# Two edits to an encoder kernel: the turns of one pair's probabilities stand ahead of the next pair's scores on TensorE, and the copies of the turned probabilities wait for the values of the pair before

## The chip, the core and the metric

The kernel runs on one core of a Trainium2 chip. TensorE (PE in the profile) multiplies matrices, PEld is its weight load, VectorE (DVE) and ScalarE (ACT) work on tiles in on-chip memory and on the accumulator banks, GpSimd (POOL) does a few small operations, and SyncE (SP) issues most of the DMAs. The metric is the device time of one execution in microseconds (us), lower is better.

## What is computed

The reference is a two-layer encoder trunk for 256 positions of width 1024 in float32. Cut to what matters here:

```python
for l in range(DEPTH):                       # DEPTH = 2
    x = x + 0.5 * swiglu(rmsnorm(x, g_ff1[l]), w1_ff1[l], w3_ff1[l], w2_ff1[l])
    h = rmsnorm(x, g_mix[l])
    p = h @ w_in[l]                          # queries, keys, values of three branches, and three gates
    o_a = diff_attention(...)                # 4 heads: softmax(s0) - lam * softmax(s1), then values, then a norm
    o_b = neighborhood_attention(...)        # 8 heads
    o_c = dilated_attention(...)             # 8 heads
    g = sigmoid(gates)
    merged = g[0] * (o_a @ w_br_a[l]) + g[1] * (o_b @ w_br_b[l]) + g[2] * (o_c @ w_br_c[l])
    x = x + merged @ w_o[l]
    x = x + 0.5 * swiglu(rmsnorm(x, g_ff2[l]), w1_ff2[l], w3_ff2[l], w2_ff2[l])
return rmsnorm(x, g_final)
```

Each attention is scores, a bias, a softmax over 256 keys, and the product of the probabilities with the values.

## The kernel before

All weights come as a stream of 1 MB units of 128 x 2048 numbers. To keep float32 precision, ScalarE copies each unit to a rounded high part (`to_hi`, L445, `whi`), VectorE subtracts it from the original to get the low part (`to_lo`, L1102, `wlo`), and TensorE forms each product from three matmuls, high by high, high by low and low by high (`three`, L679 to L681). Three units are in flight. The order of the instructions on each engine is written out by hand, and semaphores are all that joins the engines. Each engine works through its list strictly in that order.

The change lies in the mixing stage, which each layer runs once. Its loop over `j` has one unit per step: `MIX` lists 18 of them (gates and branch projections), four output units follow. Beside the units of steps 0 to 13 the stage handles the attention in 12 pairs of heads: pairs 0 to 3 are the dilated branch C, 4 to 7 the neighbourhood branch B, and 8 to 11 the differential branch A (there one "pair" is one head with its two softmaxes). TensorE's step `j` before the change is:

- the unit of the step (`unit_rows`, 24 matmuls of 512 columns),
- `scores(j)`: the scores of pair j into banks 2 and 3,
- `values(j - 2)`: the product of the turned probabilities of pair j-2 with its values,
- `turn_probs(j - 1)`: the transposes of pair j-1's normalised probabilities into banks 4 and 5 (eight transposes, four for each head of the pair; four in all for a pair of branch A).

ScalarE's step `j` has, in this order: in some steps two gate activations (L617); `pair_to_hi(j + 1)` (L564, `hTh_last`, waits for the end of `scores(j)`, since it writes the tiles that they read); `to_hi` of a unit three steps ahead (L445); the copies of pair j-1's turned probabilities (L629, `pTh`, two for branches C and B, one for A); the high part of pair j-1's values (L634, `hTh`); and the four exponentials of pair j (L641, `probs`). VectorE's step `j` has: in some steps work on the branch products; `add_bias(j)` (L1326); the low part of pair j+1 (L1255); the low parts of the turned probabilities of pair j-1 (L1353, `pTl`) and of its values (L1356); `to_lo` of the unit (L1102); the reciprocal of pair j's softmax sums (L1393); and the normalisation of pair j's probabilities (four of L1399, the first two for the first head; for branch A two of L1406 and two of L1410). The transposes of a head wait for its normalisation (`normed`, or `mixed` for A), and those of pairs 1 to 8 for the low parts of the pair before (`pT_split`), which still read the same banks.

`values(j - 2)` reads the copies of pair j-2. The copies of pair j-1 overwrite them. Before the change they wait for `probs_turned` alone, which TensorE raises behind the values.

Of the kernel before, what the change touches and what calls it, by code (L numbers as in the profile page):

```python
# [46 lines left out]
PAIRS = 12  # L47
# [50 lines left out]
def build(nc, x_in, stream, params_in, lam_in, g_final, t5_table, rpb, c_ident, c_mask, c_onehot, c_lncount, out):  # L98
    with ExitStack() as ctx:
# [117 lines left out]
        def n_norm(l, j):  # L217
            return l * 3 + (j + 1)
# [213 lines left out]
        def _(act):  # L432
# [138 lines left out]
            for l in range(DEPTH):  # L571

                later_quarters(l, 0, U_FFN1 + 2)
                ffn(l, 0, U_FFN1, 0, 1)

                later_quarters(l, 1, U_QKV + 2)
                act.wait_ge(rstd_ready, n_norm(l, 1))

                def branch(b):
                    for p in range(3):  # L580
                        u = U_QKV + 2 * p
                        to_hi(l, u + 3, b * 2)
                        if p == 0:
                            for t in range(TILES):
                                if t == 0:
                                    act.wait_ge(half_done, n_unit(l, u + 1, b * 2))
                                else:
                                    act.wait_ge(unit_used, n_unit(l, u + 1, b * 2) + CREDIT)
                                act.activation(v[:, b, t, :], v_bank(b, t)[:, :], ACT.Copy, scale=rstd[:, 0, t:t + 1]).then_inc(v_out, 1)
                        else:  # L590
                            for blk in range(BLK):
                                if blk == 0:
                                    act.wait_ge(half_done, n_unit(l, u + 1, b * 2))
                                elif blk == 2:
                                    act.wait_ge(unit_used, n_unit(l, u + 1, b * 2) + CREDIT)
                                half = qk_bank(b, p - 1, blk)[:, S:2 * S]
                                act.activation(qkT[:, b, p - 1, blk, :], half if p == 1 else half[:, ::-1], ACT.Copy).then_inc(qk_half, 1)
                        to_hi(l, u + 4, b * 2)

                branch(0)  # L600
                act.wait_ge(setup_done, 4)
                act.wait_ge(t5_stored, 16)
                pair_to_hi(l, 0)
                for b in (1, 2):
                    branch(b)
                act.activation(warm[:, :], factors[:, 0, :], ACT.Exp)

                for j in range(len(MIX) + 4):
                    u = U_MIX + j
                    kind, b, n, a = MIX[j] if j < len(MIX) else ("wo", 0, 0, 0)  # L610
                    if kind == "gate" and a == 1:
                        for t in range(TILES):
                            if t == 0:
                                act.wait_ge(half_done, n_unit(l, u))
                            else:
                                act.wait_ge(unit_used, n_unit(l, u) + CREDIT)
                            act.activation(gate[:, b % 2, t, n * 512:(n + 1) * 512], bank[t][:, :], ACT.Tanh,  # L617
                                           scale=rstd[:, 1, t:t + 1]).then_inc(gate_ready, 1)
                    if j < PAIRS - 1:
                        pair_to_hi(l, j + 1)  # L620
                    for inst, q in QUARTERS_AT.get(j, []):
                        quarter(l, inst, q)
                    due = split_at(u) if j < len(MIX) + 3 else []
                    for w in due[:1]:
                        to_hi(l, w)
                    if 1 <= j <= PAIRS:
                        for m in range(2 if j <= 8 else 1):
                            act.wait_ge(probs_turned, n_probs_turned(l, j - 1, m))
                            act.activation(pTh[:, m, :, :] if j <= 8 else pTa[:, :, :], bank[4 + m][:, :].rearrange("p (a b) -> p a b", a=2),  # L629
                                           ACT.Copy).then_inc(pT_hi, 1)  # L630
                    if 1 <= j <= 8:
                        if j > 1:
                            act.wait_ge(pv_done, l * 12 + j - 1)
                        act.activation(map_columns(vh[:, :, :]), v_of_pair(j - 1), ACT.Copy).then_inc(v_hi, 1)  # L634
                    if j < PAIRS:
                        if j >= 1:
                            act.wait_ge(probs_turned, n_probs_turned(l, j - 1, 0 if j - 1 >= 8 else 1))
                        for m in range(2):
                            act.wait_ge(biased, l * 24 + 2 * j + m + 1)
                            for t in range(TILES):  # L640
                                e = act.activation(probs[:, m, t, ::-1], sneg[:, m, t, :], ACT.Exp, scale=-1.0,  # L641
                                                   bias=negmax[:, m, t:t + 1], accum_out=den[:, m, t:t + 1])
                            e.then_inc(exp_done, 1)
                    for b2, half in OT_AT.get(j, []):
                        if b2 == BA:
                            act.wait_ge(o_turned, l * 2 + half + 1)
                        else:
                            act.wait_ge(pv_done, l * 12 + 4 * b2 + 2 * half + 2)
                        if b2 == BB:
                            act.wait_ge(unit_used, n_unit(l, U_MIX + 9) + CREDIT)  # L650
                        dst, src = o_parts(b2, half)[0], o_turns(b2, half)
                        act.activation(dst, src, ACT.Copy, **({"scale": params[:, l, SUBLN:SUBLN + 1]} if b2 == BA else {})).then_inc(o_hi, 1)
                    for w in due[1:]:
                        to_hi(l, w)

                later_quarters(l, 3, U_FFN2 + 2)
                if l == DEPTH - 1:
                    act.dma_start(gate[:, 0, 0, :], bass.AP(g_final.tensor, 0, [[0, P], [1, D]])).then_inc(gfin_landed, 16)
                ffn(l, 1, U_FFN2, 2, NEXT)
# [16 lines left out]
        def _(pe):  # L676
# [240 lines left out]
            for l in range(DEPTH):  # L917
# [58 lines left out]
                def turn_probs(s):  # L976
                    b = s // 4
                    if 1 <= s <= 8:
                        pe.wait_ge(pT_split, l * 16 + 2 * s)
                    elif s:  # L980
                        pe.wait_ge(pT_hi, n_probs_turned(l, s - 1, 0))
                    for m in range(1 if b == BA else 2):
                        if b == BA:
                            pe.wait_ge(mixed, l * 4 + (s - 8) + 1)
                        else:
                            pe.wait_ge(normed, l * 16 + 2 * s + m + 1)
                        for kb in range(TILES):
                            for t in range(TILES):
                                last = pe.transpose(bank[4 + m][:, kb * S + t * P:kb * S + (t + 1) * P],  # L989
                                                    probs[:, m, t, kb * P:(kb + 1) * P], ident[:, :])  # L990
                        last.then_inc(probs_turned, 1)
# [46 lines left out]
                for j, (kind, b, n, a) in enumerate(MIX):  # L1038
                    pr = product_banks(j)
                    before = products_read(j) if j and a == 0 else (None, None)  # L1040
                    if kind == "gate":
                        unit_rows(l, U_MIX + j, 0, xTh, xTl, 4 * a, pr, a == 0, a == 1, before=before)
                    else:
                        if n == 0:
                            pe.wait_ge(o_split, l * 6 + 2 * b + 2)
                        th, tl, k0 = (xTh, xTl, 4) if b == BA else (oTh, oTl, 0)
                        turn_first = (lambda: turn_quarter(l, 2, 0)) if (b, n) == (BA, 1) else None
                        unit_rows(l, U_MIX + j, 0, th, tl, k0, pr, True, True, before=before, mid=turn_first)
                    if j < PAIRS:
                        scores(j)  # L1050
                    if 2 <= j < PAIRS + 2:
                        values(j - 2)
                    if 1 <= j <= PAIRS:
                        turn_probs(j - 1)
                    if j == PAIRS + 2:
                        turn_o(0)
                        turn_o(1)
# [507 lines left out]
```

## Time and profile before

| | |
|---|---|
| median of 3 runs | 1285.77 us (1285.12 to 1286.24) |
| profiled execution | 1284.99 us |
| its span, first to last instruction | 1282.7 us |
| TensorE busy | 1270.0 us (99%) |
| weight load busy | 1082.0 us (84%) |
| VectorE busy | 867.7 us (68%) |
| ScalarE busy | 681.4 us (53%) |
| mixing stage of the first layer with pairs in it | from 298 to 405 us of the span |
| the same of the second layer | from 931 to 1038 us |

In the rows below a time at the start of a row is the start in us from the beginning of the span, the next number is how long the row's instructions took together, and "x8" says that the row stands for eight of them. A matmul's end is modelled, and matmuls overlap, so on TensorE the distance from one start to the next says more than the length of one. A note such as "[0.75 <-ACT pTh L629]" says that the engine sat idle for 0.75 us before the row, until ScalarE had done line L629.

### The profile page before, as it was taken

The page shows a single profiled execution, that of the slowest core. Times are in us where ns is not written, and L with a number is a line of the kernel's source. Part 1 is how long each engine was busy: PE and PEld are TensorE (multiplying, and loading weights), DVE is VectorE, ACT ScalarE, POOL GpSimd, SP SyncE. Part 2 cuts the span into 40 slices and gives each one's busy share as a digit, 9 for nine tenths or more (in the row PEclk, how much of TensorE's full clock was granted, in tenths as well). Part 3 has the DMA queues.
Part 4 walks back from the last instruction along what each step waited for, and adds up shares of the span by engine and source line. Part 5 has one row for each costly group of instructions (what it writes and reads, how often), then busy time and mean ns, then how long its engine had stood idle before and what let it go on. Part 6 is the DMA issues. An engine that isn't in the chain of part 4 may idle for free.

```text
span 1282.7 us, 17691 instructions
## 1 busy us (share of the span) xinstructions
PE 1270.0 (99%) x6825; PEld 1082.0 (84%) x6825; DVE 867.7 (68%) x1236; ACT 681.4 (53%) x919; POOL 42.2 (3%) x56
## 2 busy tenths in 40 slices
PE   8999999999999999999999999999999999999997
PEld 6888888888888888888888888888888888888886
DVE  6666667556988775666676665765578887655665
ACT  6445555445765454544555445554477653645444
POOL 0411100000000000000000000000000000000000
PEclk9999999999999999999999999999999999999999
DMA  8787855564645545555455555455555345555550
GB/s 287 238 258 239 259 212 197 196 214 148 230 122 177 180 179 196 182 183 187 171 194 196 196 184 180 160 211 193 188 195 207 123 171 190 181 197 196 196 191 39
DMA packets 59356, 245.13 MB, mean 191 GB/s; under 512 B 21360, under 2 KB 27760, under 8 KB 32552
## 3 DMA queue, kind: packets, MB, share of 16 engines
q1 hardware_dynamic: 58160, 242.83, 54.6%
q10 hardware_dynamic: 1112, 1.57, 0.4%
q8 instruction: 35, 0.57, 0.2%
q14 instruction: 17, 0.14, 0.0%
q0 software_dynamic: 32, 0.02, 0.0%
HBM read 239.14 MB, written 5.27 MB: 191 GB/s over the span
## 4 chain that ended last, share of the span: by engine, by line
PE 96%; DVE 2%; ACT 1%; DMA 1%; issue 0%; SPq 0%; POOL 0%; POOLq 0%; ACTq 0%; DVEq 0%
PE bank L745 30%; PE bank L679 16%; PE bank L749 15%; PE bank L681 15%; PE bank L680 15%; PE bank L989 1%; PE bank L803 1%; PE bank L1003 1%; DVE wlo L1102 1%; DMA raw<-in_stream 1%; ACT whi L445 0%; PE bank L707 0%; PE bank L699 0%; DVE h L1161 0%; DVE h L1169 0%
## 5 line engine op out<-in xcount | busy, mean ns | idle before, releaser
L1102 DVE TENSOR_TENSOR wlo<-raw,whi 128x2048 fp32r<-128x2048 f32 x209 | 479.1, 2294 | 276.5 <-ACT whi L445 272.6
L445 ACT ACTIVATE whi<-raw 128x2048 fp32r<-128x2048 f32 x209 | 398.7, 1911 | 225.7 <-PE bank L749 142.2
L745 PE MATMUL bank<-xT,whi 128*128 128x512 f32 x1664 | 414.8, 391 | 0.0
L745 PEld LDWEIGHTS bank<-xT,whi 128*128 128x128 f32 x1664 | 301.8, 188 | 55.7 <-DVE wlo L1102 0.9
L749 PEld LDWEIGHTS bank<-xT,wlo 128*128 128x128 f32 x1664 | 220.2, 190 | 12.8
L749 PE MATMUL bank<-xT,wlo 128*128 128x256 f32 x1664 | 224.1, 282 | 0.0
L679 PE MATMUL bank<-whi,xT 128*128 128x512 f32 x432 | 171.7, 397 | 0.0
L681 PE MATMUL bank<-whi,xT 128*128 128x512 f32 x432 | 168.5, 390 | 0.0
L680 PE MATMUL bank<-wlo,xT 128*128 128x512 f32 x432 | 168.3, 390 | 0.0
L679 PE MATMUL bank<-whi,hTh 128*128 128x512 f32 x320 | 124.6, 390 | 0.0
L680 PE MATMUL bank<-wlo,hTh 128*128 128x512 f32 x320 | 124.5, 389 | 0.0
L681 PE MATMUL bank<-whi,hTl 128*128 128x512 f32 x320 | 124.5, 389 | 0.0
L681 PEld LDWEIGHTS bank<-whi,xT 128*128 128x128 f32 x432 | 81.1, 188 | 17.4
L680 PEld LDWEIGHTS bank<-wlo,xT 128*128 128x128 f32 x432 | 81.2, 188 | 16.0
L679 PEld LDWEIGHTS bank<-whi,xT 128*128 128x128 f32 x432 | 81.2, 188 | 15.9
L499 ACT ACTIVATE h<-bank 128x256 f32<-128x256 f32 x80 | 26.4, 382 | 87.8 <-PE bank L745 87.8
L680 PEld LDWEIGHTS bank<-wlo,hTh 128*128 128x128 f32 x320 | 60.1, 188 | 12.8
L679 PEld LDWEIGHTS bank<-whi,hTh 128*128 128x128 f32 x320 | 60.1, 188 | 12.6
L681 PEld LDWEIGHTS bank<-whi,hTl 128*128 128x128 f32 x320 | 60.1, 188 | 12.5
L1161 DVE TENSOR_TENSOR h<-bank,h 128x256 f32<-128x256 f32 x80 | 30.2, 419 | 43.9 <-ACT h L499 43.9
L503 ACT ACTIVATE silu<-silu 128x512 f32<-128x512 f32 x40 | 25.3, 633 | 51.4 <-DVE silu L1164 51.4
L641 ACT ACTIVATE probs<-sneg,negmax 128x256 f32<-128x256 f32 x96 | 47.5, 501 | 0.6 <-DVE negmax L1326 0.6
(162 smaller groups left out, 1139.8 us busy)
## 6 DMA issues: line engine op xcount, KB each, us to landing
raw<-in_stream SPq DMA_DIRECT2D x209, 1024.0 KB, 4.8
bias<-t_rows SPq DMA_DIRECT2D x24, 256.0 KB, 6.5
bias<-in_rpb SPq DMA_DIRECT2D x16, 256.0 KB, 7.7
masked<-bias SPq DMA_DIRECT2D x8, 512.0 KB, 6.9
bias<-masked SPq DMA_DIRECT2D x8, 512.0 KB, 4.7
raw<-in_stream SPq DMA_DIRECT2D x11, 256.0 KB, 7.4
x<-in_x SPq DMA_DIRECT2D x4, 256.0 KB, 6.2
gate<-in_g_final ACTq DMA_DIRECT2D x1, 512.0 KB, 3.6
```

The lines of the kernel that those rows point to most:

```text
L445: act.activation(whi[:, s, :], raw[:, s, :], ACT.Copy).then_inc(hi_ready, 1)
L499: act.activation((h_flat if blk >= 2 else silu_flat)[:, part], bank[4 + blk][:, S:2 * S], ACT.Copy).then_inc(half_copied, 1)
L503: act.activation(silu_flat, silu_flat, ACT.Silu).then_inc(silu_done, 1)
L641: e = act.activation(probs[:, m, t, ::-1], sneg[:, m, t, :], ACT.Exp, scale=-1.0, bias=negmax[:, m, t:t + 1], accum_out=den[:, m, t:t + 1])
L679: pe.matmul(dst, sh, mh, start=start, stop=False)
L680: pe.matmul(dst, sh, ml, start=False, stop=False)
L681: return pe.matmul(dst, sl, mh, start=False, stop=stop)
L745: return pe.matmul(dst[blk][:, :], whi[:, s, w], xT[:, 4 * a + k, :, :].rearrange("p a s -> p (a s)"), start=start, stop=stop)
L749: return pe.matmul(dst[blk][:, 0:S], wlo[:, s, w], xT[:, 4 * a + k, 0, :], start=False, stop=stop)
L803: last = pe.transpose(bank[6 + q % 2][:, k * P:(k + 1) * P], src[:, t, c:c + P], ident[:, :])
L1102: dve.tensor_tensor(wlo[:, s, :], raw[:, s, :], whi[:, s, :].bitcast(F32), ALU.subtract).then_inc(unit_split, 1)
L1161: dve.tensor_tensor(sums, bank[4 + blk][:, 0:S], sums, ALU.add).then_inc(summed, 1)
```

## The change

On TensorE `turn_probs(j - 1)` moves from the end of the step to the place between the unit and `scores(j)`. Since `probs_turned` then no longer says that `values(j - 2)` is done, ScalarE gets one more wait ahead of the copies: from step 2 on it waits until `pv_done` counts the values of pair j-2. Nothing is added or removed on TensorE, VectorE, GpSimd or SyncE.

```diff
@@ scalar, mixing loop @@
                     if 1 <= j <= PAIRS:
+                        if j >= 2:
+                            act.wait_ge(pv_done, l * 12 + j - 1)
                         for m in range(2 if j <= 8 else 1):
                             act.wait_ge(probs_turned, n_probs_turned(l, j - 1, m))
@@ tensor, mixing loop @@
+                    if 1 <= j <= PAIRS:
+                        turn_probs(j - 1)
                     if j < PAIRS:
                         scores(j)
                     if 2 <= j < PAIRS + 2:
                         values(j - 2)
-                    if 1 <= j <= PAIRS:
-                        turn_probs(j - 1)
```

From ScalarE's edit on, every line number of the changed file is two higher.

On TensorE, in step 2 of the first layer, the rows before are these, with repeated rows left out: the last matmul of the unit (reading `xT`), the scores (reading `hTh_last`), the values (reading `pTh`), the eight transposes (reading `ident` and `probs`) and the first matmul of the next unit.

```order
L681 MATMUL bank<-whi,xT 128x512
L679 MATMUL bank<-hTh_last 128x256
L680 MATMUL bank<-hTl_last,hTh_last 128x256
...
L679 MATMUL bank<-pTh,hTh 128x256
L680 MATMUL bank<-pTl,hTh 128x256
...
L989 MATMUL bank<-ident,probs 128x128 x8
L679 MATMUL bank<-whi,xT 128x512
```

In the changed kernel the same place reads as follows.

```order
L683 MATMUL bank<-whi,xT 128x512
L991 MATMUL bank<-ident,probs 128x128 x8
L681 MATMUL bank<-hTh_last 128x256
L682 MATMUL bank<-hTl_last,hTh_last 128x256
...
L681 MATMUL bank<-pTh,hTh 128x256
L682 MATMUL bank<-pTl,hTh 128x256
...
L681 MATMUL bank<-whi,xT 128x512
```

The transposes have moved up past 12 matmuls of the scores and 12 of the values.

On ScalarE the order of the rows is the same. In step 3 of the first layer it is, in the changed kernel: the high part of the next pair, the unit's high part, the two copies of the turned probabilities, the high part of the values, and the exponentials.

```order
L564 ACTIVATE hTh_last<-qkT 128x512 [waits scores_ready]
L445 ACTIVATE whi<-raw 128x2048 [waits raw_landed2,unit_used]
L631 ACTIVATE pTh<-bank 128x512 [waits probs_turned,pv_done]
L631 ACTIVATE pTh<-bank 128x512 [waits probs_turned]
L636 ACTIVATE hTh<-v 128x2x2x64 [waits pv_done]
L643 ACTIVATE probs,den<-sneg,negmax 128x256 [waits biased,probs_turned]
```

Only the first copy has changed: before, its wait was for `probs_turned` alone.

## Rows read from the trace of the kernel before

**Rows 1.** The page: busy us of each engine, share of the span, instructions.

```profile
PE 1270.0 (99%) x6825; PEld 1082.0 (84%) x6825; DVE 867.7 (68%) x1236; ACT 681.4 (53%) x919; POOL 42.2 (3%) x56
```

**Rows 2.** Busy time in the first layer's mixing stage: start:end, length, PE, PEld, DVE, ACT, POOL, granted clock, DMA.

```profile
295.00:405.00 110.00, 110.00 (x674) 92.17 (x672) 92.96 (x257) 78.00 (x168) 0.00 (x0) 1.00 0.51 170
```

**Rows 3.** Timeline of TensorE, steps 4 and 5 of the first layer.

```profile
335.16 0.39 PE L679 MATMUL bank<-hTh_last 64*128 64x256 f32 x2
...
336.07 0.39 PE L679 MATMUL bank<-pTh,hTh 128*128 128x256 f32 x1
...
337.61 1.03 PE L989 MATMUL bank<-ident,probs 128*128 128x128 f32 x8
338.40 0.47 PE L679 MATMUL bank<-whi,xT 128*128 128x512 f32 x1
...
343.72 0.39 PE L681 MATMUL bank<-whi,xT 128*128 128x512 f32 x1
344.04 0.39 PE L679 MATMUL bank<-hTh_last 64*128 64x256 f32 x2
```

**Rows 4.** Timeline of ScalarE in the same stretch.

```profile
336.22 0.63 ACT L564 ACTIVATE hTh_last<-qkT 128x512 fp32r<-128x512 f32 x1 [3.14 <-PE bank L681]
336.75 1.90 ACT L445 ACTIVATE whi<-raw 128x2048 fp32r<-128x2048 f32 x1
338.56 1.07 ACT L629 ACTIVATE pTh<-bank 128x512 fp32r<-128x512 f32 x2
```

**Rows 5.** Timeline of VectorE in the same stretch.

```profile
339.17 1.29 DVE L1353 TENSOR_TENSOR pTl<-bank,pTh 128x512 fp32r<-128x512 f32 x2 [0.75 <-ACT pTh L629]
...
343.11 1.14 DVE L1399 TENSOR_SCALAR probs<-probs,rden 128x256 f32<-128x256 f32 x4
```

**Rows 6.** Timeline of TensorE and VectorE, step 4 of the second layer.

```profile
968.97 0.39 PE L679 MATMUL bank<-pTh,hTh 128*128 128x256 f32 x1
976.01 1.15 DVE L1399 TENSOR_SCALAR probs<-probs,rden 128x256 f32<-128x256 f32 x4
```

**Rows 7.** Timeline behind the first feed-forward stage: TensorE waits for VectorE.

```profile
451.24 1.28 DVE L1133 SCALAR_TENSOR_TENSOR x<-bank,x 128x512 f32<-128x512 f32 x2
452.10 0.59 PEld L803 LDWEIGHTS bank<-ident,x 128*128 128x128 f32 x4
452.33 0.60 PE L803 MATMUL bank<-ident,x 128*128 128x128 f32 x4
```

**Rows 8.** Timeline of VectorE and TensorE, steps 0 to 2 of the first layer.

```profile
307.67 1.14 DVE L1399 TENSOR_SCALAR probs<-probs,rden 128x256 f32<-128x256 f32 x4
310.89 1.09 PE L989 MATMUL bank<-ident,probs 128*128 128x128 f32 x8
317.93 1.14 DVE L1399 TENSOR_SCALAR probs<-probs,rden 128x256 f32<-128x256 f32 x4
```

**Rows 9.** Timeline of TensorE, steps 8 to 11 of the first layer: the values' first matmuls, and turns.

```profile
371.59 0.39 PE L679 MATMUL bank<-pTh,hTh 128*128 128x256 f32 x1
...
380.47 0.39 PE L679 MATMUL bank<-pTh,hTh 128*128 128x256 f32 x1
...
388.91 1.16 PE L1003 MATMUL bank<-v,silu 128*128 128x128 f32 x8
389.91 0.60 PE L989 MATMUL bank<-ident,probs 128*128 128x128 f32 x4
...
396.82 1.16 PE L1003 MATMUL bank<-v,silu 128*128 128x128 f32 x8
```

**Rows 10.** Timeline of VectorE, steps 8 to 11: the second half of branch A's normalisation.

```profile
379.41 0.88 DVE L1410 SCALAR_TENSOR_TENSOR probs<-probs,lrden 128x256 f32<-128x256 f32 x2
...
386.24 0.88 DVE L1410 SCALAR_TENSOR_TENSOR probs<-probs,lrden 128x256 f32<-128x256 f32 x2
...
395.26 0.88 DVE L1410 SCALAR_TENSOR_TENSOR probs<-probs,lrden 128x256 f32<-128x256 f32 x2
...
402.56 0.88 DVE L1410 SCALAR_TENSOR_TENSOR probs<-probs,lrden 128x256 f32<-128x256 f32 x2
```

## Prediction

> **What bounds the kernel now.** I read the page first. TensorE is busy for 1270.0 us of the 1282.7 us span [rows 1]. Then the busy time of the stage that the change touches: in 110 us of the first layer's mixing stage TensorE is busy for 110.00, VectorE for 92.96 and ScalarE for 78.00, at a granted clock of 1.00, the 2.4 GHz level [rows 2]. So nothing that waits today is waited for by TensorE, and the change takes no work off it. It can only add waits on TensorE, or save the small losses between one kind of matmul and the next. The question is therefore when the normalised probabilities are ready, against the new, earlier place of their transposes. For that I went through the timeline of the three engines step by step.
>
> Some names. S is the start of the first instruction behind a step's scores on TensorE, in most steps the first matmul of the values. N is the end of the normalisation of the first head of the same pair. In step 4, S is 336.07 [rows 3]. VectorE starts the four normalisations at 343.11, and they take 1.14 together [rows 5]; one is about 0.35 long and they start 0.265 apart (0.35 + 3 x 0.265 = 1.14), so the first two end at 343.11 + 0.61 = 343.72, and the second two 0.53 later. N - S is 343.72 - 336.07 = 7.65.
>
> What sets these 7.65 us? ScalarE makes the next pair's high part right when the scores are done, 0.15 after S (336.22, after 3.14 idle). It takes a unit's high part at 336.75, and the copies of the turned probabilities start when that is done, at 338.56 [rows 4]. VectorE sits idle for 0.75 until the first copy is there, and then works through low parts, a unit's low part and the reciprocal up to the normalisation [rows 5]. So the chain starts from the end of the scores, and it is in the order of the two engines' lists, not in the turns: when ScalarE reaches the copies the turns are just done. The whole chain hangs on S and moves with it.
>
> **The change, part by part.** Nothing is added to or taken from TensorE's work. The transposes of pair j move up to a place right behind the unit of step j+1. How long after S does TensorE reach that place? Values: 337.61 - 336.07 = 1.54. The unit's 24 matmuls: the first starts at 338.40 and the 24th at 343.72, which is 23 steps of 0.23, so the next can start at 343.95, 5.55 later [rows 3]. TensorE arrives at S + 7.09. The first head's probabilities are there at S + 7.65, later. In the kernel before, the scores and values of step j+1 lie in between, and the turns start 2.45 us later than the unit's end (scores 336.07 - 335.16 = 0.91, values 1.54 [rows 3]); this is what hid the chain.
>
> What does the engine lose on top when it really waits? The row of a wait for VectorE elsewhere: two residual sums take 1.28 together (about 0.68 each, overlapping), the first ends at 451.92, the weight load of the turn that waits for it starts at 452.10 and its first matmul at 452.33 [rows 7]. That is 0.41 from the end of the VectorE instruction. The two bounds are 0.18 (only the way of the signal, if the load is hidden) and 0.41; I take 0.41, since a turn loads its own data and that row is the same kind of wait. The second head's four turns could start at N + 0.41 + 0.40 (eight take 0.79 [rows 3]), but their data end at N + 0.53, and 0.41 on top is N + 0.94: another 0.13.
>
> Now each pair of a layer:
> - Pair 0: its first step has no values and no copies, so it is normalised at 307.67 + 1.14 = 308.81. Its turns stand at 310.89 now, behind 0.91 of scores; at 309.98 they find everything ready [rows 8]. 0.
> - Pair 1: S was 310.89, the start of the turns then in that place, and N is 317.93 + 0.61 = 318.54 [rows 8], again 7.65. There are no values in step 1, so TensorE arrives after the unit alone: 7.65 + 0.41 + 0.13 - 5.55 = 2.64 us.
> - Pairs 2 to 7, six of them: 7.65 + 0.41 + 0.13 - 7.09 = 1.10 each, 6.60 in all.
> - Pair 8, the first of branch A: its normalisation has two stages, the last of which ends at 379.41 + 0.88 = 380.29; S is 371.59 [rows 9, 10], so 8.70. One wait only: 8.70 + 0.41 - 7.09 = 2.02.
> - Pair 9: 386.24 + 0.88 - 380.47 = 6.65 [rows 9, 10]; with 0.41 it is 7.06, just under the 7.09. 0.
> - Pair 10: 395.26 + 0.88 - 388.91 = 7.23. The values of branch A are shorter, 389.91 - 388.91 = 1.00 [rows 9, 10], so TensorE arrives at 6.55: 7.23 + 0.41 - 6.55 = 1.09.
> - Pair 11: 402.56 + 0.88 - 396.82 = 6.62 [rows 9, 10]: 6.62 + 0.41 - 6.55 = 0.48.
>
> The sum is 12.83 us a layer. The second layer reads the same: in its step 4 the chain is 976.01 + 0.61 - 968.97 = 7.65 [rows 6]. So 25.7 us.
>
> The waits don't pile up on one another, and none pays for the next: behind each the scores follow, a new S starts a new chain of the same length, and TensorE again has 7.09 us of work for it. Nothing behind the stage can give the time back, since TensorE is never waiting there for anything that this delay would hide.
>
> ScalarE's new wait costs nothing by these rows: the values now end 1.54 after S, and ScalarE reaches the copies 2.49 after S (338.56 - 336.07 [rows 3, 4]), so there is 0.95 to spare, 0.77 after the 0.18 that a signal takes. What hides it is the copy of the unit's high part, which ScalarE does from 0.68 to 2.49 after S; without that it would wait about 1 us (0.68 against 1.72). Queued behind it are the exponentials, and with them the normalisation. The transposes also wait for the low parts of the pair before, but those are made ahead of the normalisation on VectorE's list, so they are never last. SyncE's loads wait for units that are freed; with TensorE slower there is only more room.
>
> The small losses between kinds of matmuls: 0.32 instead of 0.23 from the unit's last matmul to the scores [rows 3], so 0.09 there, and the like behind a turn. Turned differently, they may save or cost about 0.1 a step, at 12 steps and two layers up to 2.4 us either way. I take 0, since in most steps TensorE is waiting at just that place.
>
> **The clock.** The granted clock was at the upper level in this stage, with TensorE never idle in it [rows 2]. Now it will be idle for about 1 us of every 10, and no row here shows what follows from that. The Trainium skill (page "TensorE: Matmul & The Clock Gate", section "HAM oscillation — how this bites in real kernels") says that pauses between bursts of matmuls can bring the clock down to its lower level. By that rule the stage would run at the price of the third rival below; by the rows it costs 25.7 us.
>
> **Rivals.** First, the chain gets shorter, and nothing changes. The exponentials of pair j wait for the turns of pair j-1, and the copies too. If it is the turns that ScalarE waits for, they come 2.45 us earlier, N - S falls well under 6.68 (7.09 - 0.41, the point from which it decides), and almost no wait is left: N - S would be 5.20, which leaves 5.20 + 0.54 - 5.55 = 0.19 at pair 1 and nothing elsewhere, 1286 us. Against it: the copies start right behind the unit's high part [rows 4], not behind the turns. Second, the other side: no waits, and the small losses fall away since turns follow a unit and the values lead into the next one. With 0.09 saved at both places in 11 steps of two layers that is 22 x 0.18 = 4.0, so 1282 us. It needs the same condition, N - S below 6.68, at each pair. Third, the clock goes to 1.2 GHz in the stage. A step would then have 2 x 7.09 = 14.2 us of work beside the chain, no wait, and with turns and scores (2 x 1.7) be 17.6 long in place of 8.9: some 8.7 x 22 = 190 us, 1475 us. Fourth, the waits are there, but without the 0.23 of the first load and the 0.13 of the second head: 12.83 - 10 x 0.23 - 7 x 0.13 = 9.6 a layer, 19 in all, 1304 us.
>
> **How the numbers follow.** The forecast, waits of the size above: 0.72. The cheaper waits (fourth): 0.16. No change (first): 0.06. Faster (second): 0.03. Clock (third): 0.02. The remaining 0.01 I leave to anything else that is slower. The sum stands against the profiled execution's 1284.99: 1284.99 + 25.7 = 1310.7. The median of the runs is 0.8 above that execution, so 1311.5, and I say 1311. For the range I go from the cheap waits with 2.4 saved between kinds, 1285.8 + 19.2 - 2.4 = 1302.6, to 1311.5 + 2.4 and a little for waits that are not listed, 1315: 1302 to 1315, which leaves out less than 2 in 10. 0.2% of this kernel's time, about 2.6 us, is what a measurement can tell from no change. Faster by more than that 0.03, within it 0.06, slower 0.91.
>
> **What would show it.** In the profile after, TensorE's list of waits should have the turns of `probs` waiting for VectorE's normalisation, about ten times a layer, the longest in step 2 (some 2.5 us) and step 9 (some 2), about 1 us in steps 3 to 8, and hardly any in steps 1 and 10. N - S should still be 7.65. A step in the middle should be about 10.0 us from scores to scores where it was 344.04 - 335.16 = 8.88 [rows 3], TensorE's clock should stay at 1.00, and ScalarE should not be waiting for the values at its copies, except in step 9. The prediction is wrong if N - S shrinks, if TensorE's re-entry after a wait is far from 0.41, or if the clock drops.

## The result, and the profile after

The changed kernel takes 1309.94 us (median of 4 runs, 1308.53 to 1310.51), the kernel before beside it 1286.01 us. The ratio is 1.0185 (95% interval 1.0172 to 1.0197): 23.9 us slower. The forecast was 1311. The profiled execution took 1310.3 us, its span 1308.0, which is 25.3 more than before.

The page of the changed kernel, busy time of the engines, against [rows 1]:

```profile
span 1308.0 us, 17713 instructions
...
PE 1278.8 (98%) x6825; PEld 1085.6 (83%) x6825; DVE 868.0 (66%) x1236; ACT 681.4 (52%) x919; POOL 42.5 (3%) x56
```

TensorE has the same 6825 matmuls, but its idle time has risen from 12.7 to 29.2 us, and its busy time by 8.8: a matmul drawn 0.39 long hides the first 0.16 us of a wait behind it (348.74 + 0.39 = 349.13 in the rows below, where the next could start at 348.97), and some matmuls ran at a lower clock, as shown further down. Where it idles is in its list of waits (us in total, times, longest):

```profile
PE bank L991 <- DVE probs L1401: 12.1, 14, 2.1
PE bank L991 <- DVE probs L1412: 4.8, 4, 1.7
PE bank L805 <- DVE x L1135: 1.6, 3, 0.5
```

The first two are new: the turns wait for the normalisation, 18 times in the two layers, 16.9 us. The two longest of a layer, those of pair 1 and pair 8, are these, with the scores behind them (first layer):

```profile
311.77 0.39 PE L681 MATMUL bank<-hTh_last 64*128 64x256 f32 x2
...
320.49 1.09 PE L991 MATMUL bank<-ident,probs 128*128 128x128 f32 x8 [2.07 <-DVE probs L1401]
321.51 0.39 PE L681 MATMUL bank<-hTh_last 64*128 64x256 f32 x2
...
380.97 0.39 PE L681 MATMUL bank<-pTh,hTh 128*128 128x256 f32 x1
...
389.82 0.63 PE L991 MATMUL bank<-ident,probs 128*128 128x128 f32 x4 [1.69 <-DVE probs L1412]
390.38 0.39 PE L681 MATMUL bank<-hTh_last 64*128 64x256 f32 x2
...
400.30 0.39 PE L681 MATMUL bank<-hTh_last 64*128 64x256 f32 x2
```

Step 4 to 5 of the first layer shows one of the short ones, TensorE first, then VectorE, then ScalarE; the rows answer to [rows 3 to 5].

```profile
341.05 0.39 PE L681 MATMUL bank<-hTh_last 64*128 64x256 f32 x2
...
341.96 0.39 PE L681 MATMUL bank<-pTh,hTh 128*128 128x256 f32 x1
...
343.50 0.40 PE L681 MATMUL bank<-whi,xT 128*128 128x512 f32 x1
...
348.74 0.39 PE L683 MATMUL bank<-whi,xT 128*128 128x512 f32 x1
349.77 1.09 PE L991 MATMUL bank<-ident,probs 128*128 128x128 f32 x8 [0.64 <-DVE probs L1401]
350.79 0.39 PE L681 MATMUL bank<-hTh_last 64*128 64x256 f32 x2
```

```profile
345.06 1.29 DVE L1355 TENSOR_TENSOR pTl<-bank,pTh 128x512 fp32r<-128x512 f32 x2 [0.75 <-ACT pTh L631]
349.01 1.14 DVE L1401 TENSOR_SCALAR probs<-probs,rden 128x256 f32<-128x256 f32 x4
```

```profile
342.11 0.63 ACT L564 ACTIVATE hTh_last<-qkT 128x512 fp32r<-128x512 f32 x1 [4.07 <-PE bank L683]
342.65 1.90 ACT L445 ACTIVATE whi<-raw 128x2048 fp32r<-128x2048 f32 x1
344.46 1.06 ACT L631 ACTIVATE pTh<-bank 128x512 fp32r<-128x512 f32 x2
```

S is 341.96, N is 349.01 + 0.61 = 349.62, and N - S is 7.66, as it was. ScalarE still comes to the copies 2.50 after S and waits for nothing there. The unit is done at about 348.97, the turns start at 349.77. From scores to scores the step is 350.79 - 341.05 = 9.74 us, where it was 8.88.

There is a second thing, which the forecast gave a chance of 0.02 as a state of the whole stage: the clock does fall, but for a short time. The stretch around the turns of pair 8 in the first layer (columns as in [rows 2], the granted clock third from the end):

```profile
388.00:390.00 2.00, 0.31 (x3) 0.21 (x3) 1.95 (x6) 0.00 (x0) 0.00 (x0) 1.00 0.55 94
390.00:392.00 2.00, 2.00 (x19) 1.60 (x18) 1.25 (x4) 0.46 (x1) 0.00 (x0) 0.77 0.97 410
392.00:394.00 2.00, 2.00 (x11) 2.00 (x11) 1.74 (x10) 0.18 (x1) 0.00 (x0) 0.50 0.85 122
394.00:396.00 2.00, 2.00 (x10) 1.67 (x10) 0.00 (x0) 1.63 (x6) 0.00 (x0) 0.87 0.96 304
```

TensorE idled from 388.1 to 389.8. About 1.3 us after it had started again its clock went to 0.50, the 1.2 GHz level, and came back about 3.4 us later. In the second layer the same place reads 0.55 and 0.59 (1036 to 1040). Everywhere else in the two stages it is 1.00. One more such stretch lies at the start of the span, long before the change: the rows here are the changed kernel and, under it, the kernel before.

```profile
10.00:12.00 2.00, 2.00 (x6) 1.44 (x6) 1.60 (x3) 0.90 (x2) 0.00 (x0) 0.50 1.05 388
10.00:12.00 2.00, 1.99 (x9) 1.37 (x8) 1.48 (x3) 0.62 (x2) 0.00 (x0) 1.00 1.04 397
```

### The profile page after: what moved, and what is told of

Its sections match the earlier page's. It is cut to its first block, busy times and chain, and to the rows that moved or that the text cites. A ratio compares the mean times of both kernels' runs of the same rounds, so it can differ in the third digit from the quotient of the medians.

```text
span 1308.0 us, 17713 instructions
## 1 busy us (share of the span) xinstructions
PE 1278.8 (98%) x6825; PEld 1085.6 (83%) x6825; DVE 868.0 (66%) x1236; ACT 681.4 (52%) x919; POOL 42.5 (3%) x56
## 4 chain that ended last, share of the span: by engine, by line
PE 86%; DVE 8%; ACT 3%; issue 2%; DMA 0%; ACTq 0%; POOL 0%; POOLq 0%; DVEq 0%
PE bank L747 29%; PE bank L751 15%; PE bank L681 13%; PE bank L683 12%; PE bank L682 12%; DVE wlo L1104 4%; PE bank L991 2%; ACT whi L445 2%; DVE pTl L1355 2%; PE bank L805 1%; ACT pTh L631 1%; DVE probs L1401 1%; PE bank L1005 0%; DMA raw<-in_stream 0%; DVE hTl L1358 0%
## 5 line engine op out<-in xcount | busy, mean ns | idle before, releaser
L683 PEld LDWEIGHTS bank<-whi,hTl 128*128 128x128 f32 x320 | 60.1, 188 | 12.7
L503 ACT ACTIVATE silu<-silu 128x512 f32<-128x512 f32 x40 | 25.3, 632 | 49.9 <-DVE silu L1166 49.9
L564 ACT ACTIVATE hTh_last<-qkT 128x512 fp32r<-128x512 f32 x24 | 15.2, 632 | 67.5 <-PE bank L683 67.5
```

The source lines that it names most:

```text
L503: act.activation(silu_flat, silu_flat, ACT.Silu).then_inc(silu_done, 1)
L683: return pe.matmul(dst, sl, mh, start=False, stop=stop)
```

## The experiments

Nine kernels were run. Each was measured beside the kernel before (medians of 1285.9 to 1286.3).

**ScalarE's wait alone.** The kernel before, with the two added lines of ScalarE, TensorE's order untouched.

```diff
+                        if j >= 2:
+                            act.wait_ge(pv_done, l * 12 + j - 1)
```

> The kernel before with only ScalarE's new wait for the values ahead of the copies; TensorE's order as before. If the time comes from the place of the turns (the chain from the scores to the normalised probabilities is longer than TensorE's work in between), this is the kernel before: 1286 us, within 1 us, since in that order the turns end behind the values anyway. If it is the added wait itself that holds ScalarE up, this run shows the loss, 1300 us or more.

Measured: 1285.63 us, ratio 0.9998 (0.9989 to 1.0008). The wait costs nothing where it is already met, as it always is in that order: the turns stand behind the values. That it costs nothing in the changed order too is not shown by this run; the run with both passes behind, below, shows it.

**The unit's low part behind the normalisation.** The changed kernel, on VectorE:

```diff
-                    for w in due[:1]:
-                        to_lo(l, w)
+                    if j >= PAIRS:
+                        for w in due[:1]:
+                            to_lo(l, w)
                     ...
-                    for w in due[1:]:
+                    for w in due[1 if j >= PAIRS else 0:]:
                         to_lo(l, w)
```

> The changed kernel, but VectorE makes a unit's low part (2.3 us) behind the normalisation of the pair in steps 1 to 11, not ahead of it. If the chain from the scores sets the waits, N - S falls from 7.65 to about 6.7, the waits of pairs 2 to 7 vanish (TensorE needs 7.16 us to come to the turns), and pairs 1, 8 and 10 keep about 1.2, 0.9 and 0.5: 2.6 us of waits a layer in place of 9.3, and some 1295 us. If the waits hang on something else (the turns' own place, ScalarE's wait), the time stays near 1310.

Measured: 1292.6 us, ratio 1.0054 (1.0037 to 1.0071). TensorE's waits for the normalisation in it:

```profile
PE bank L991 <- DVE probs L1413: 2.3, 4, 0.7
PE bank L991 <- DVE probs L1402: 2.2, 2, 1.1
```

The 14 waits of the first kind are two (pair 1 in each layer, 1.1), and the four of branch A are down from 4.8 to 2.3 us. In step 4 the normalisation now starts at S + 6.06, where it was S + 7.05, and the turns follow the unit without idling:

```profile
337.55 0.39 PE L681 MATMUL bank<-hTh_last 64*128 64x256 f32 x2
...
338.46 0.39 PE L681 MATMUL bank<-pTh,hTh 128*128 128x256 f32 x1
...
345.47 1.03 PE L991 MATMUL bank<-ident,probs 128*128 128x128 f32 x8
346.43 0.39 PE L681 MATMUL bank<-hTh_last 64*128 64x256 f32 x2
```

One pass of 2.3 us taken out of the chain on another engine gave back 17.3 of the 23.9 us. The chain is 0.99 us shorter, not 2.3, since VectorE now waits 1.12 us for ScalarE's exponentials ahead of the reciprocal. So it is this chain that TensorE waits for. The step is 346.43 - 337.55 = 8.88 us, as in the kernel before.

**Both passes behind.** As above, and the same edit for `to_hi` on ScalarE.

> As the run before, and ScalarE too makes the unit's high part behind the exponentials in steps 1 to 11. The chain then has neither of the two unit passes in it: N - S about 5.9, no wait of TensorE left but some 0.1 us at pair 8. What is left against the kernel before is then only the price of another order of kinds of matmuls on TensorE, read from the changed kernel's trace as about 0.16 us in each of 12 steps, 1.9 us a layer: 1290 us. If that price is no real one, 1286; if the chain is not what TensorE waits for, near 1310.

Measured: 1286.44 us, ratio 1.0007 (0.9998 to 1.0017). No wait for a normalisation is left in the list of waits; only at pair 8 do the turns still start 0.14 us late, 0.15 after the end of theirs. In step 4 the turns start 7.00 after S, where TensorE comes to them:

```profile
336.39 0.39 PE L682 MATMUL bank<-hTh_last 64*128 64x256 f32 x2
...
337.30 0.38 PE L682 MATMUL bank<-pTh,hTh 128*128 128x256 f32 x1
...
344.30 1.04 PE L992 MATMUL bank<-ident,probs 128*128 128x128 f32 x8
345.27 0.39 PE L682 MATMUL bank<-hTh_last 64*128 64x256 f32 x2
```

The step from 336.39 to 345.27 is 8.88 us, exactly that of the kernel before. So the 3.8 us that I expected to be left for another order of kinds of matmuls are not there. What the turns lose in front of the scores (0.97 us to them, where it was 0.79 to the unit) the unit saves in front of the turns (5.47 to them, where it was 5.64 to the scores).

This run also prices ScalarE's new wait. Without the unit's high part ahead of them the copies do wait for the values:

```profile
ACT pTh L632 <- PE bank L684: 11.9, 14, 1.0
```

These are 14 waits of up to 1.0 us on ScalarE, and the time is that of the kernel before.

**The control: both passes behind, in the kernel before.**

> The kernel before, with the unit's high part behind the exponentials on ScalarE and its low part behind the normalisation on VectorE in steps 1 to 11, TensorE's order as before. TensorE waits for nothing in the stage in either, so a chain that is 2 us shorter is worth nothing there: 1286 us, within 1. If those two passes cost TensorE anything today, it is faster, 1283 or less.

Measured: 1286.31 us, ratio 1.0001 (0.9991 to 1.0010). A shorter chain is worth nothing where TensorE does not wait for it; in the changed kernel the same edit was worth 23.5 us.

**Pair 8 back in its old place.**

```diff
-                    if 1 <= j <= PAIRS:
+                    if 1 <= j <= PAIRS and j != 9:
                         turn_probs(j - 1)
                     ...
+                    if j == 9:
+                        turn_probs(j - 1)
```

> The changed kernel with the turns of pair 8 alone back behind the values of step 9. If waits are local (each new end of scores starts its own chain), this saves that pair's wait of 1.70, its 0.16 of another order, and the 1.3 us of the lower clock behind it, 3.2 us a layer: 1303.6 us. If the clock falls anyway at another of the waits, 1306.3. If the waits pile up or pass on to the next pair, less is saved, 1308 or more.

Measured: 1303.94 us, ratio 1.0143 (1.0127 to 1.0158), 6.0 us less than the changed kernel. The waits are local: taking one away leaves the others as they were. Pair 9, the next one, still turns without a wait, pair 10's wait is 0.76 (0.70 in the changed kernel), and the steps of pairs 2 to 7, ahead of it, are the same 9.73 to 9.80 us.

**Pairs 1 and 8 back**, the two with the long waits (`j not in (2, 9)` in the place of `j != 9`).

> The changed kernel with the turns of pairs 1 and 8, those with the two long waits (2.2 and 1.7 us), back behind the values; the others stay early. By the waits of the changed kernel's trace 6 pairs at 0.87, pair 10 at 0.9 and pair 11 at 0.3 are left, 6.4 us a layer, and if only long waits bring the clock down, it stays at 1.00 in the stage: 1286 + 12.9 = 1299 us. If the clock falls behind waits of 0.9 us too, some 1.5 us more a layer and a granted clock of about 0.996 over the span, 1302.

Measured: 1297.52 us, ratio 1.0092 (1.0075 to 1.0109), 1.5 less than expected, in part because pair 2's step now waits less (0.18 idle, where it was 0.64): it takes 10.15 us with eight turns more in it. The longest wait is 0.7, and the granted clock is 1.00 in all of the two stages.

**TensorE kept busy in pair 8's wait**, to price the clock by itself:

```diff
+                    if s == 4 * BA:
+                        for _ in range(6):
+                            pe.matmul(bank[5][:, :], xTh[:, 0, 0:P], xT[:, 0, :, :].rearrange("p a s -> p (a s)"), start=True, stop=True)
```

> The changed kernel with six more matmuls of 512 columns into an unused bank on TensorE ahead of the turns of pair 8 (step 9 of each layer), where it waits 1.70 us; their results are used by nothing. If the clock falls to its lower level behind that wait because TensorE is idle in it, the granted clock stays at 1.00 there and some 1.3 us a layer come back: 1307.3 us. If the clock falls for another reason, the time stays at 1310 and the clock still falls there.

Measured: 1308.6 us, ratio 1.0175 (1.0158 to 1.0192). The median is 1.3 us lower in place of 2.6, with runs from 1306.87 to 1309.43, which overlap those of the changed kernel, so the time alone shows nothing. The profile shows more: behind pair 8 the clock stays up, and the step from 390.92 to 399.37 is 8.45 us, as before, where the changed kernel had 400.30 - 390.38 = 9.92.

```profile
390.92 0.39 PE L681 MATMUL bank<-hTh_last 64*128 64x256 f32 x2
...
399.37 0.39 PE L681 MATMUL bank<-hTh_last 64*128 64x256 f32 x2
```

But now it falls behind pair 1, whose wait of 2.1 us was there in the changed kernel too and was not followed by a fall in that profile:

```profile
318.00:320.00 2.00, 0.34 (x2) 0.37 (x3) 1.97 (x6) 0.00 (x0) 0.00 (x0) 0.95 0.21 33
320.00:322.00 2.00, 2.00 (x11) 1.67 (x12) 0.04 (x1) 0.00 (x0) 0.00 (x0) 0.50 0.86 311
322.00:324.00 2.00, 2.00 (x18) 1.78 (x16) 0.77 (x6) 0.85 (x2) 0.00 (x0) 0.70 0.95 277
```

**TensorE kept busy in both long waits** (eight such matmuls at pair 1, six at pair 8).

> The changed kernel with idle time of TensorE filled by matmuls of 512 columns whose results are used by nothing, ahead of the turns of pair 1 (eight matmuls, 1.8 us of a wait of 2.2) and of pair 8 (six, 1.4 of 1.7). The waits stay, but TensorE is busy in them. If idling is what brings the clock down, it stays at 1.00 in both places and the time is 1310 - 2 x 1.5 = 1307 us. If it falls all the same behind one of the waits, 1308.6 as with one place filled.

Measured: 1307.63 us, ratio 1.0167 (1.0150 to 1.0183), 2.3 less than the changed kernel, 3 expected; the two intervals overlap, so this too rests on the profile. The same places:

```profile
320.00:322.00 2.00, 1.83 (x12) 1.17 (x10) 1.40 (x6) 0.00 (x0) 0.00 (x0) 1.00 0.43 74
322.00:324.00 2.00, 2.00 (x22) 1.79 (x21) 0.79 (x7) 0.87 (x2) 0.00 (x0) 1.00 0.96 401
388.00:390.00 2.00, 2.00 (x10) 1.36 (x8) 1.93 (x7) 0.00 (x0) 0.00 (x0) 1.00 0.18 25
390.00:392.00 2.00, 1.76 (x18) 1.40 (x18) 1.44 (x3) 0.06 (x1) 0.00 (x0) 1.00 0.94 381
```

The clock is at 1.00 at both, and in all four runs its mean over the span is 0.998, where the changed kernel's four had 0.995 to 0.997. The chain and the places of the turns are those of the changed kernel. Over the profiles, none of the six filled waits was followed by a fall of the clock (two of `filler`, four here), and four of the eight long ones left unfilled were (two of four in the changed kernel, both in `filler`, none of two with pair 8 back). That fits a clock that follows TensorE's idling; since half of the unfilled waits had no fall either, it is not proof.

**Values ahead of the scores.** The kernel before, with `values(j - 2)` ahead of `scores(j)` and the turns last.

> The kernel before with the values ahead of the scores in each step, turns last as before: unit, values, scores, turns. By the chain there is no wait (TensorE has 8.9 us of work from the end of one step's scores to the turns, against 7.8), so only the order of kinds of matmuls counts: 0.1 us a step either way at most, 1283.6 to 1288.4 us. If each order had the same losses, 1286.

Measured: 1286.37 us, ratio 1.0002 (0.9993 to 1.0011). Another order of the same kinds of matmuls is free where it brings hardly any wait (0.5 us in all here, steps of 8.84 us), as in the run with both passes behind. No run was faster than the kernel before by more than its interval.

## Why the prediction was right, and where its terms were off

The mechanism was right. N - S stayed as it was (7.66) with the turns 2.45 us of TensorE's work earlier, TensorE waited where it was said to, the runs that shorten the chain take the loss away, and the run with ScalarE's wait alone doesn't make it. The places were right too: none at pairs 0 and 9, the longest at pairs 1 and 8. But the size, 25.7 for a measured 23.9 of the medians and 25.3 of the spans, is right in part by luck, because two errors partly cancel: the waits were taken too dear and the clock at nothing. Of the three signs of being wrong that the prediction named, N - S did not shrink, but TensorE's re-entry was far from 0.41, and the clock dropped. Per layer, from the starts of the rows:

| | forecast | measured | from |
|---|---|---|---|
| pair 1 | 2.64 | 2.34 | step 1 to 2: 9.74, before 7.40 |
| pairs 2 to 7 | 6.60 | 5.25 | steps of 9.73 to 9.80, before 8.88 to 8.90 |
| pair 8 | 2.02 | 1.84 | 389.82 is S + 8.85, unhindered S + 7.01 |
| pair 10 | 1.09 | 0.86 | turns at S + 7.35, unhindered at S + 6.49 |
| pair 11 | 0.48 | 0.31 | turns at S + 6.77, unhindered at S + 6.46 |
| clock | 0 | 1.47 | step 9: 9.92, with filled wait 8.45 |
| sum | 12.83 | 12.07 | whole stage: 113.81, before 101.60, so 12.21 |

"Unhindered" is the run with both passes behind, first layer; for pair 8, which is still a little late there, it is the place of pair 7. Two layers give 24.4 of the 25.3 us; the other 0.9 lie ahead of the first scores, which start at 304.28 and before at 303.37, in a stretch that the change doesn't touch. They go with the low clock of the rows at 10 to 12 us: in the eleven profiles the first scores start at 304.00 to 304.87 in the four that have it and at 303.34 to 303.67 in the others, whatever the order of the turns. So 24.4 is what the change cost in this profile.

**The mis-sized step is the cost of a wait.** The prediction took 0.41 us from the end of the VectorE instruction to the first turn, from [rows 7], and 0.13 for the second head. Measured it is 349.77 - 349.62 = 0.15, and the second head costs 0.05 (turns and all take 1.02 to the scores, and 0.97 where nothing waits). Against that, TensorE comes to the turns 0.09 earlier than the prediction had it, at S + 7.00 in place of 7.09. The row was misread: at 452.10 TensorE was still in a matmul that started at that time and goes on for 0.23, and the weight load of the turn ran beside it. The turn at 452.33 is late for that reason, not because of a wait. The row of TensorE just ahead of it shows this:

```profile
452.10 0.39 PE L681 MATMUL bank<-whi,xT 128*128 128x512 f32 x1
```

So the fourth rival, waits without those two terms, 19 us in all, was nearer the truth for the waits' size: 10.6 a layer, 21.2 in all, measured by steps (the 16.9 of the list leave out the 0.16 that each wait hides, the waits of pair 11 and those of the second heads).

**The term put at nothing is the clock.** The prediction had it as all or nothing and gave it 0.02. In the changed kernel's profile it falls behind a long wait for some 3.4 us, once a layer, and that costs 1.5 us. The rule of the Trainium skill that the prediction weighed (page "TensorE: Matmul & The Clock Gate", section "HAM oscillation — how this bites in real kernels") agrees with the trace in its kind: the clock came to the lower level behind pauses, here of 1.7 and 2.1 us (0.50 in the rows above), which are shorter than the waits of that section's example.

**The costs put at nothing** were nothing: ScalarE's wait (1.0007 with 11.9 us of it), the order of kinds of matmuls (8.88 us a step in either order). In step 9 the copies did wait for the values, as was said, and longer than expected, 2.19 us at the slow clock, but its pair had the room. Pair 3's chain was 0.25 longer before (VectorE was still at another unit), which the prediction's one figure for pairs 2 to 7 passes over; it lost that: its reciprocal comes 6.89 after S, before 7.14.

## What to carry to other kernels

In this kernel TensorE is the bound and hardly ever waits, and no other order of its work gained anything (1.0007 and 1.0002 where it brought hardly any wait, 1.0185 where it brought many). What counted is how long the operand's chain through the other engines is, against TensorE's work between the two ends of that chain. With both measured from the same event, here the end of the scores, the sign and most of the size of this reordering followed before it was run. The remedy for such a wait is on the chain: passes that nobody waits for yet belong behind the ones that TensorE needs next, and that was worth 23.5 us in the changed kernel and nothing in the kernel before.

## What was not expected of the hardware

A wait of TensorE of 1.7 to 2.1 us in an otherwise dense stretch can be followed by about 3.4 us at the lower clock (0.50). In the four cases seen it began 0.1 to 1.3 us after the engine was busy again. It did not follow every such wait: in the changed kernel's profile the wait of 2.07 us at pair 1 was not followed by a fall and that of 1.69 at pair 8 was, in both layers; with pair 8's wait filled it was pair 1's, in both layers. In the profile of the kernel with pair 8 back, which has pair 1's wait, none fell. With waits up to 1.1 us none was seen. What decides between the long ones stays open.

A turn that waits for VectorE started 0.15 us after the instruction that it waits for had ended, weight load included (349.62 to 349.77, where TensorE had nothing else in progress).
